# A two-layer hybrid decoder step on one core: value rows turned by transposes instead of products with the identity, retention's sample queries from a masked pair of columns, its chunk states from one full-width product

## What is computed

```python
# retention, a prompt, chunks of 128 (heads of 64 keys, 128 values)
scores = einsum('bhik,bhjk->bhij', qb, kb) * decay
o = einsum('bhij,bhjv->bhiv', scores, vb) + einsum('bhik,bhkv->bhiv', qb * q_dec, s)
s = s * c_dec + einsum('bhjk,bhjv->bhkv', kb * k_dec, vb)
# for a sample (one token) the same is: s = gamma * s + k v^T ; o = q s
# SSD, a sample: s = exp(da) * s + dt * x B^T ; y = C s
# RMSNorm: y = x * rsqrt(mean(x*x) + EPS) * g      (all fp32)
```

## Time and profile before

| | |
|---|---|
| median of 3 runs | 2827.82 us (2823.33, 2827.82, 2830.88) |
| span of the profiled execution | 2827.9 us |
| PE busy | 2740.2 us, 97% |
| DVE, POOL, ACT busy | 1965.8, 1270.2, 858.8 us |
| chain that ended last | PE 42%, issue 23%, POOL 20%, DVE 10%, DMA 3% |

### The profile page before, as it was taken

One profiled execution on the slowest core, in us unless ns is written; L12 is line 12 of the kernel. 1 busy time (PEld: TensorE's weight loads), 2 busy tenths in 40 slices (PEclk: granted clock), 3 DMA queues, 4 the chain that ended last, 5 costly groups with the idle time before them and its releaser, 6 DMA issues.

```text
span 2827.9 us, 51809 instructions
## 1 busy us (share of the span) xinstructions
PE 2740.2 (97%) x19158; PEld 2676.5 (95%) x19158; DVE 1965.8 (70%) x2460; ACT 858.8 (30%) x1368; POOL 1270.2 (45%) x732
## 2 busy tenths in 40 slices
PE   9999999989899999999999999998998999999997
PEld 8999999989899999999999999998898999999997
DVE  7658896367877666667846598854588666667777
ACT  4333231124322223223413342311243223233233
POOL 2333233212566566666433333231126566666662
PEclk9999999999999999999999999999999999999998
DMA  4325334410111111111223343344111111111112
GB/s 161 132 68 166 125 102 167 136 55 31 46 54 52 52 45 45 52 52 45 71 83 102 113 135 134 96 171 145 33 37 48 51 45 45 52 52 45 47 58 88
DMA packets 76410, 228.63 MB, mean 81 GB/s; under 512 B 18736, under 2 KB 19888, under 8 KB 75200
## 3 DMA queue, kind: packets, MB, share of 16 engines
q1 hardware_dynamic: 71888, 211.25, 22.7%
q10 hardware_dynamic: 4368, 15.33, 1.7%
HBM read 181.10 MB, written 45.96 MB: 80 GB/s over the span
## 4 chain that ended last, share of the span: by engine, by line
PE 42%; issue 23%; POOL 20%; DVE 10%; DMA 3%; ACT 1%; POOLq 1%; DVEq 0%; SPq 0%; ACTq 0%
POOL sb_w_lo L800 13%; PE ps L897 12%; PE ps L898 11%; PE ps L899 11%; DMA sb_w_raw<-w 2%; POOL sb_w_raw L843 2%; POOL sb_wsum L832 2%; DVE sb_pt L1877 2%; POOL sb_w_raw L839 1%; DVE sb_x L1867 1%; POOL sb_rawx L835 1%; POOL sb_w_raw L835 1%; PE ps L1009 1%; DMA sb_raw<-proj 1%; PE ps L1126 1%
## 5 line engine op out<-in xcount | busy, mean ns | idle before, releaser
L800 POOL TENSOR_TENSOR sb_w_lo<-sb_w_raw,sb_w_hi 128x512 fp32r<-128x512 f32 (+1 forms) x348 | 635.0, 1827 | 505.9 <-ACT sb_w_hi L1682 497.2
L897 PE MATMUL ps<-sb_p_hi,sb_w_hi 128*128 128x258 f32 (+1 forms) x2528 | 732.7, 290 | 25.2 <-POOL sb_w_lo L800 13.1
L899 PE MATMUL ps<-sb_p_hi,sb_w_lo 128*128 128x258 f32 (+1 forms) x2528 | 727.0, 288 | 0.0
L898 PE MATMUL ps<-sb_p_lo,sb_w_hi 128*128 128x258 f32 (+1 forms) x2528 | 726.9, 288 | 0.0
L797 POOL TENSOR_TENSOR sb_w_hi<-sb_w_raw,sb_ones 128x1024 fp32r<-128x1024 f32 (+1 forms) x92 | 180.6, 1963 | 917.2 <-PEq L894 826.2
L897 PE MATMUL ps<-sb_h_hi,sb_w_hi 128*128 128x344 f32 x1632 | 533.8, 327 | 3.5 <-DVE sb_h_lo L1836 1.9
L898 PE MATMUL ps<-sb_h_lo,sb_w_hi 128*128 128x344 f32 x1632 | 523.0, 320 | 0.0
L899 PE MATMUL ps<-sb_h_hi,sb_w_lo 128*128 128x344 f32 x1632 | 521.6, 320 | 0.0
L897 PEld LDWEIGHTS ps<-sb_p_hi,sb_w_hi 128*128 128x128 f32 x2528 | 479.4, 190 | 31.0 <-POOL sb_w_lo L800 19.5
L897 PE MATMUL ps<-sb_y_hi,sb_w_hi 128*128 128x344 f32 x1440 | 479.2, 333 | 24.6 <-DVE sb_x L1867 14.3
L898 PEld LDWEIGHTS ps<-sb_p_lo,sb_w_hi 128*128 128x128 f32 x2528 | 481.0, 190 | 0.0
(11 more groups left out here) (301 smaller groups left out, 3697.8 us busy)
## 6 DMA issues: line engine op xcount, KB each, us to landing
sb_w_raw<-w SPq DMA_DIRECT2D x178, 512.0 KB, 3.6
proj<-sb_ev SPq DMA_DIRECT2D x64, 516.0 KB, 3.0
sb_rawx<-w SPq DMA_DIRECT2D x44, 512.0 KB, 3.5
sb_pt<-proj SPq DMA_DIRECT2D x28, 516.0 KB, 5.0
sb_raw<-proj SPq DMA_DIRECT2D x16, 516.0 KB, 4.4
sb_raw<-proj ACTq DMA_DIRECT2D x16, 516.0 KB, 4.2
sb_ch<-cumT SPq DMA_DIRECT2D x32, 256.0 KB, 3.9
sb_raw<-ssd_state SPq DMA_DIRECT2D x4, 1024.0 KB, 6.3
```

Of the source, the lines that this page charges most:

```text
L800: return nc.gpsimd.tensor_tensor(o, a, h.bitcast(F32), ALU.subtract)
L897: mm(o, wh, ah, start=first, stop=False)
L898: mm(o, wh, al, start=False, stop=False)
L899: return mm(o, wl, ah, start=False, stop=last)
```

## The change

Four edits: (1) products with the identity become transposes in `spread_rstd`, `decode_s`, `tail` and the last spread; (2) the values of the samples are first widened by ACT (two activations in a retention unit, behind chunk 3) into `raw[:, 1]`, and turned by 8 full-width transposes; (3) the sample outputs come from 8 products with all 128 rows and a pair of masked query columns, which DVE prepares (a memset and two copies) after `dec_pe` 1; (4) the addition to the state is one product of all 128 key columns with both heads' values, of which DVE takes each head's half in two updates, now ahead of the gating of the outputs.

```diff
+    qs = small[:, 32:48].rearrange("p (b h) -> p b h", h=2)
@@ spread_rstd (and the same in the last spread) @@
-                ins = mm(o, rt[0:n, c:c + 1].to_broadcast([n, P]), ident[0:n, 0:n], start=True, stop=True)
+                ins = nc.tensor.transpose(o, rt[0:n, c:c + 1].to_broadcast([n, P]), ident[0:n, 0:n])
@@ b_ret @@
-            for h in range(2):
-                ins = mm(ps[64 * h:64 * h + 64, 4 + c % 2, 384:512], kd(c)[:, 64 * h:64 * h + 64], vg(c)[:, 128 * h:128 * h + 128],
-                         start=True, stop=True)
-            ins.then_inc(*sg.on("b_done", (u, c)))
+            mm(ps[:, 6, 256:512], kd(c), vg(c)[:, 0:256], start=True, stop=True).then_inc(*sg.on("b_done", (u, c)))
@@ decode_s, for k in range(2), for b in range(DEC) @@
-                    ins = mm(abf[:, b * 128:(b + 1) * 128], pt[:, k, SEQ + b:SEQ + b + 1].to_broadcast([P, P]),
-                             ident, start=True, stop=True)
+                    ins = nc.tensor.transpose(abf[:, b * 128:(b + 1) * 128],
+                                              pt[:, k, SEQ + b:SEQ + b + 1].to_broadcast([P, P]), ident)
@@ decode_r @@
             pe.wait_ge(*sg.after("bwork", (u, NCH - 1)))
+            pe.wait_ge(*sg.after("v_wide", u))
             for b in range(DEC):
-                for h in range(2):
-                    v = pt[:, X0[u] + h, SEQ + b:SEQ + b + 1].to_broadcast([P, 64])
-                    ins = mm(abf[64 * h:64 * h + 64, b * 128:(b + 1) * 128], v, ident, start=True, stop=True)
+                n = slice(b * 128, (b + 1) * 128)
+                ins = nc.tensor.transpose(abf[:, n], raw[:, 1, n], ident)
...
-            for h in range(2):
-                for b in range(DEC):
-                    q = slice(64 * h, 64 * h + 64)
-                    ins = mm(ab[:, h, b:b + 1], raw[q, 0, b * 128:(b + 1) * 128],
-                             pt[q, 0, SEQ + b:SEQ + b + 1], start=True, stop=True)
+            for b in range(DEC):
+                ins = mm(ab[:, 0, 2 * b:2 * b + 2], raw[:, 0, b * 128:(b + 1) * 128], qs[:, b, :], start=True, stop=True)
@@ tail @@
-                ins = mm(ps[0:8, 6, 128 * n:128 * n + 128], pt[:, j, d], ident, start=True, stop=True)
+                ins = nc.tensor.transpose(ps[0:8, 6, 128 * n:128 * n + 128], pt[:, j, d], ident)
@@ ACT, called in a retention unit behind square_r(u, 3) and root_table(u) @@
+        def widen_values(u):
+            act.wait_ge(*sg.after("rope_done", u))
+            act.wait_ge(*sg.after("v_loaded", (u, 1)))
+            for h in range(2):
+                wide = raw[:, 1, 0:1024].rearrange("p (b h n) -> p b h n", b=DEC, h=2)[:, :, h, :]
+                ins = af(wide, pt[:, X0[u] + h, d].unsqueeze(2).to_broadcast([P, DEC, 64]), ACT.Identity)
+            ins.then_inc(*sg.on("v_wide", u))
@@ DVE, b_work_r @@
+            for h in range(2):
+                q = slice(64 * h, 64 * h + 64)
+                ins = stt(St[q, 0:128], St[q, 0:128], C("cdec", u - 4)[q], ps[q, 6, 256 + 128 * h:384 + 128 * h], ALU.mult,
+                          ALU.add)
+            ins.then_inc(*sg.on("bwork", (u, c)))
             v.tensor_tensor(pt[:, X0[u]:X0[u] + 2, cols(c)], heads(ps[:, 6, 0:256], 2), heads(vg(c)[:, 256:512], 2),
                             ALU.mult).then_inc(*sg.on("o_gated", (u, c)))
-            stt(St[:, 0:128], St[:, 0:128], C("cdec", u - 4), ps[:, 4 + c % 2, 384:512], ALU.mult,
-                ALU.add).then_inc(*sg.on("bwork", (u, c)))
@@ DVE, decode_r, behind dec_pe 1 @@
+            v.memset(small[:, 32:48], 0.0).then_inc(*line.step())
+            dve.wait_ge(*line.last())
+            for h in range(2):
+                q = slice(64 * h, 64 * h + 64)
+                v.tensor_copy(qs[q, :, h], pt[q, 0, d])
...
-            v.tensor_copy(pt[:, X0[u]:X0[u] + 2, d], ab[:, :, 0:DEC]).then_inc(*sg.on("ys_ready", u))
+            v.tensor_copy(pt[:, X0[u]:X0[u] + 2, d],
+                          ab[:, 0, 0:2 * DEC].rearrange("p (b h) -> p h b", h=2)).then_inc(*sg.on("ys_ready", u))
```

More of the change, by code:

```diff
@@ L1631, in _ @@
                         root_table(u)
+                        widen_values(u)
                 if u == 4:
```

## The result

| | before | after |
|---|---|---|
| median of the paired runs | 2826.14 us (2823.33 to 2830.88, 4 runs) | 2791.37 us (2790.16 to 2793.29, 4 runs) |
| profiled execution: span | 2827.9 us | 2788.9 us (time 2791.04) |
| mean granted clock of its span | 0.986 | 0.991 |
| PE busy, records | 2740.2 us, 19158 | 2702.5 us, 18801 |
| DVE, ACT, POOL busy | 1965.8, 858.8, 1270.2 us | 1989.6, 863.1, 1266.4 us |

The ratio is 0.9878, 95% interval 0.9867 to 0.989: faster by 34.8 us, where 32.0 were forecast, and the median lies in the range of 2787 to 2811. Between the two profiled spans the difference is 39.0 us. A span is 2.1 us shorter than its time after, and 2.4 to 2.6 us shorter in the runs of the kernel before. So the execution profiled before took, by this estimate, about 2830.4 us, close to its slowest run (2830.88) and not to the median, with which its span agreed by chance.

The account below looks back on a forecast made before the run. The prediction took PE as the bound, busy 2740 of 2828 us, so time is mostly the sum of its records. Its terms summed to 32.0 us, from 2827.9 to 2795.9, forecast as a median of 2795.8 us, range 2787 to 2811.

Parts of the forecast that it names:

- spreads (988): Spread of the token scales, four times: nine records fewer at 0.11 us, 1.0 us each, 4.0 us gained.
- SSD rows (1065): Rows of the SSD samples, eight groups: eight records fewer, 0.89 us each, 7.1 us gained, PE's 0.84 us wait unchanged.
- tails (1096): Unit tails: two records fewer in each SSD unit, four in each retention unit, 2.6 us gained.
- values (1075): Values of the samples, four times: 32 records become 8, 1.1 us each, 4.4 us gained.
- sample outputs (1084): Sample outputs, four times: 16 records instead of 32, 6.0 us gained less 1.2 us of PE waiting in R0, net 4.8.
- state products (1046): Addition to the state in the retention chunks: one full-width product saves 0.13 us in 24 of 32 chunks, 3.1 us.
- end: End of the program: nine records instead of eighteen let DVE's second operation start about 0.9 us earlier.
- clock: Behind the sample outputs in three of four retention units: no fall with half the one-column records, 1.7 us each, 5.1 us.
- The price of a record: On PE: a 128-column record costs 0.11 us in products and transposes; an fp32 product is two records, a transpose one.
- collision with POOL: Ahead of R0's sample outputs: DVE's copies stand until POOL's SBUF work ends, PE idles 0.6 us, twice, 1.2 us lost.
- Rival 1: Behind each run of transposes PE's clock falls, 20 times 1.7 us, 34 us lost: 2830, no change; chance 0.05.
- Rival 3: Retention loop turns to DVE's pace, state updates taking 1.9 us beside POOL instead of 0.3: 2842 us; chance 0.03.

Follow-up runs that it names:

- the second: The changed kernel measured again without any edit: median 2793.52 us, ratio 0.9887, span 2790.5 us, 62.6 us at the low clock.

## Why the prediction was right, and where it was not

| term | forecast | from the traces | note |
|---|---|---|---|
| spreads (988), 4 | 4.0 | 4.4 | 1.10 each |
| SSD rows (1065), 8 | 7.1 | 7.3 | 0.91 each |
| tails (1096) | 2.6 | 4.2 | 0.4 in S, 0.6 in R0, 0.7 in R1 |
| values (1075), 4 | 4.4 | 4.3 | 1.07 each |
| sample outputs (1084), 4 | 4.8 | 4.9 | R0 3.34 - 1.99 - 0.39, R1 1.5 |
| state products (1046) | 3.1 | 0.4 | 0.5 gained in each R0, 0.3 lost in each R1 |
| end | 0.9 | 1.1 | |
| clock | 5.1 | 8.2 | the rest of 34.8; see below |

**The price of a record** was right for every form, the broadcast and the 8-column operand too, though not for the reason given for the tails, that it follows the 128 columns which stream: the records with one query column cost 0.104 to 0.112 each as well. In R0 the outputs take 544.49 - 542.50 = 1.99 us to DVE's copy, before 3.34, less PE's new wait of 0.39. The copies' collision with POOL was forecast at a wait of 0.6 and came to 0.39.

**The tails** were under-sized. The term took 0.11 for each record, and that is what a record costs there too. It left out the step from the last record to the split product behind it: four records 0.11 apart put the last one at 330.87, and the split product came at 331.07, 0.20 later; behind the two transposes it comes at 328.56, 0.03 later. That is 0.17 more in each of the 8 tails, 1.4 us in all.

**The state products** are the step that failed. The forecast took 24 chunks at 0.13 and excepted those in which PE "next waits for the state". The 0.13 itself was right: R0's chunks show it, and R1's do once the wait is gone. In R1 three things went otherwise. `a_ret`'s wait for the state of two chunks ago, which the forecast didn't check there, holds back the 0.13 of every chunk from the second on. The squares were to cost nothing, with 0.1 us of slack left ahead of the last chunk and a bound of 0.2; they cost 0.28 in each R1. And the state was to "come out even": the two halves take 0.71 us from DVE's start, where the forecast had 0.68, and DVE starts 0.06 later in the chunk, so the state is 0.09 late. From the last `b_ret` to the values there are 2.29 us in R0 and 2.37 in R1, before 2.20.

**The clock** was right in its mechanism in R1 (the fall goes with half the narrow records, and comes back with them) and wrong in R0, where behind 16 records it falls in some executions and not in others; and it was taken as three falls, where the whole kernel's low time moves. Over the runs in pairs the before kernel's mean granted clock was 0.985 to 0.988, the changed one's 0.988 to 0.991, so a share of the gain is systematic. How much is not settled to better than a few us: the rest of the sum is 34.8 - 26.6 = 8.2 us by the first series (26.6 is the sum of the other terms in the table), 32.5 - 26.6 = 5.9 by the second (2826.06 against 2793.52), and between the two profiled spans 12.4.

Those 12.4 can be followed in the starts of PE's split products. In each layer they move by 1.8 us where the low clock behind R0's end is shorter, by 1.7 at the fall behind R1's sample outputs, by 1.2 behind R1's end, and by 1.4 behind the wait for POOL's first split in the FFN: after, the low clock lies ahead of that wait, where POOL sets the pace and it costs nothing. Late in layer 1's FFN it is 1.4, and late in layer 2's 1.2 the other way. That makes 12.4; some waits in between come and go and about cancel. Only the 1.7 in each R1 is the fall that was forecast.

**Rival 1** asked for the clock at 0.50 behind transposes: it stood at 1.00 at 319 to 323 and behind the values and the spreads. The Trainium skill ("TensorE: Matmul & The Clock Gate", Part 4: PE-mode transpose) says that transposes don't count as PE being busy in the same way. Runs of 0.9 to 1.1 us of them among split products don't show it here. **Rival 3** asked for updates of 1.9 us; with PSUM among their inputs they took 0.34 to 0.37, beside POOL too (two in 0.71 at 608.31, within POOL's operation of 607.86 to 610.22).

The sum was nearly the result (32.0 against 34.8 and 32.5). Without the clock the forecast has 26.9 and the traces 26.6. That these are so near is luck: 2.7 us too much in the state products stand against 1.6 too little in the tails and some tenths in each of the other terms. The clock's share was some 1 to 3 us too small, and the execution decides its size.

## What to carry to other kernels

Where PE is the bound, count its records: a product of two fp32 operands that only turns or spreads data is two records, a transpose one, and the saving of 0.11 us a record is there at once if the next instruction on PE waits for nothing. Look at the step to the next product as well. When a product gets shorter, list every wait that stands behind it, the met ones too, with the slack of each: two that had been met with 0.3 and 0.8 us to spare took back in R1 more than the product gave there. When a result moves to another bank, list the waits that guarded the old place; left in, they can hold back what the move was to give. And ask of a low clock who sets the pace while it lasts: the first 3.4 us of it behind R0 cost nothing, 10.2 us there cost 1.8 to 2.0, and a single profiled execution says little about which falls belong to the kernel.

## What was not expected of the hardware

- With 32 narrow records in a row the granted clock fell to 0.50 at or behind them in 11 of 12 units (one column and 64 rows, or two columns and 128 rows); 16 did in 1 of 22 in R1 and 12 of 22 in R0.
- Two DVE copies of 64x8 from SBUF to SBUF took 0.35 us alone and 0.43 to 2.16 when they began within POOL's 2.4 us operation on SBUF: they ended 0.2 us behind it, whenever they began.
- Behind a product of two fp32 operands with 8 or 64 output rows (lines 1096, 1046 and 1075 before) the next split product started 0.20 us after the last record; behind one with 128 output rows (line 1065), and behind the transposes, the 8-column ones too, 0.03.
- A DVE update on 64 partitions takes 0.34 us, as on 128, and two of them 0.71.
- Time at the low clock differed by 9 us between two executions of one kernel, and the spans by 1.6.
